# Column units of a four-layer plus two-layer transformer: high and low activations in one 512-column matmul, pooling by its band, and a reordered conformer tail

## What is computed

```python
for i in range(4):                      # kinds: retention, conformer, stick breaking, retention
    x = x + mixer_i(rms_norm(x))
    x = x + relu(rms_norm(x) @ w1) ** 2 @ w2          # hidden width 4096
x = rms_norm(x)
for layer in range(2):                  # hybrid layers
    h = rms_norm(x)
    b, c, xa, up, q, k, v, ga, gp, gt = split(h @ w_in)
    y_a = (b * conv3(c * xa)) @ w_a_out
    y_p = grouped(mean_of_window(up, 2 | 4 | 8 | 16) - up) @ w_pool * pool_scale
    y_t = windowed_attention(q, k, v, bias, sink) @ w_attn_out
    x = x + (sigmoid(ga) * y_a + sigmoid(gp) * y_p + sigmoid(gt) * y_t) @ w_o
    gate, u = split(rms_norm(x) @ w_gu)               # 2 x 2816
    x = x + (silu(gate) * u) @ w_down
out = rms_norm(x)
# conformer: a * sigmoid(gate), a causal depthwise convolution of 31 taps, layer norm, silu, a projection
```

## Time and profile before

| what | value |
|---|---|
| three executions, median (lowest to highest) | 2462.28 us (2461.33 to 2462.77) |
| the profiled execution, its own time | 2464.05 us |
| its span, first to last instruction | 2461.8 us, so 2.2 us lie around it |
| instructions in it | 35215, of them 14772 matmuls and as many weight loads |
| busy: PE, DVE, ACT | 2380.7, 1480.9, 1115.7 us |
| mean granted TensorE clock | 0.990 of 2.4 GHz |
| HBM | 421.40 MB read, 173 GB/s over the span |

### The profile page before, as it was taken

How to read it: one execution, slowest core, us unless ns; L and a number is a source line. 1 busy time by engine, 2 the same in 40 slices (tenths; PEclk the granted TensorE clock), 3 DMA queues, 4 the chain that set the end, 5 groups by cost and what they waited for, 6 DMA issues and landing times.

```text
span 2461.8 us, 35215 instructions
## 1 busy us (share of the span) xinstructions
PE 2380.7 (97%) x14772; PEld 2112.3 (86%) x14772; DVE 1480.9 (60%) x1443; ACT 1115.7 (45%) x1107; POOL 135.7 (6%) x182
## 2 busy tenths in 40 slices
PE   7999999979999899999999999999999999999998
PEld 6787998958988689877879978899899898998997
DVE  6666546966456654576564556755654567466454
ACT  5444444235436543454453445533444455334343
POOL 0000090500000000000000000000000000000000
PEclk9999999989999999999999999999999999999999
DMA  6443654214453255434545444435444454443543
GB/s 261 180 188 142 230 218 171 103 69 177 171 204 137 103 201 205 172 155 165 194 182 205 171 160 180 161 130 214 167 172 187 171 197 167 155 192 147 201 169 121
DMA packets 68369, 424.17 MB, mean 172 GB/s; under 512 B 10832, under 2 KB 11120, under 8 KB 22432
## 3 DMA queue, kind: packets, MB, share of 16 engines
q1 hardware_dynamic: 58752, 399.83, 42.0%
q0 software_dynamic: 9504, 22.71, 2.9%
HBM read 421.40 MB, written 5.28 MB: 173 GB/s over the span
## 4 chain that ended last, share of the span: by engine, by line
PE 90%; DVE 6%; ACT 3%; issue 1%; DMA 0%; POOL 0%; DVEq 0%; ACTq 0%
PE pair L695 19%; PE pair L697 18%; PE pair L696 18%; PE acc L695 10%; PE acc L696 9%; PE acc L697 9%; DVE work L1940 2%; DVE w_lo L1652 1%; PE pair L738 1%; PE acc L1067 1%; PE acc L1094 1%; PE acc L1083 1%; PE pair L1131 1%; ACT act_hi L1240 1%; PE pair L864 1%
## 5 line engine op out<-in xcount | busy, mean ns | idle before, releaser
L1652 DVE TENSOR_TENSOR w_lo<-raw,w_hi 128x2048 fp32r<-128x2048 f32 (+1 forms) x404 | 860.8, 2161 | 226.2 <-ACT w_hi L1185 225.2
L1185 ACT ACTIVATE w_hi<-raw 128x2048 fp32r<-128x2048 f32 (+1 forms) x404 | 713.1, 1804 | 156.3 <-PE acc L697 126.0
L695 PE MATMUL pair<-act_hi,w_hi 128*128 128x256 f32 x2496 | 709.9, 284 | 2.5 <-DVE w_lo L1652 2.5
L697 PE MATMUL pair<-act_hi,w_lo 128*128 128x256 f32 x2496 | 706.3, 283 | 0.0
L696 PE MATMUL pair<-act_lo,w_hi 128*128 128x256 f32 x2496 | 706.2, 283 | 0.0
L695 PEld LDWEIGHTS pair<-act_hi,w_hi 128*128 128x128 f32 x2496 | 478.7, 192 | 10.6 <-issue 8.5
L696 PEld LDWEIGHTS pair<-act_lo,w_hi 128*128 128x128 f32 x2496 | 478.8, 192 | 2.1
L697 PEld LDWEIGHTS pair<-act_hi,w_lo 128*128 128x128 f32 x2496 | 478.7, 192 | 0.0
L695 PE MATMUL acc<-w_hi,hid_hi 128*128 128x512 f32 x848 | 335.4, 396 | 6.2 <-DVE hid_lo L1705 6.2
L696 PE MATMUL acc<-w_lo,hid_hi 128*128 128x512 f32 x848 | 331.3, 391 | 0.0
L697 PE MATMUL acc<-w_hi,hid_lo 128*128 128x512 f32 x848 | 330.6, 390 | 0.0
(11 more groups left out here) (225 smaller groups left out, 2436.8 us busy)
## 6 DMA issues: line engine op xcount, KB each, us to landing
raw<-weights SPq DMA_DIRECT2D x356, 1024.0 KB, 6.6
raw<-weights SPq DMA_DIRECT2D x48, 512.0 KB, 6.3
work<-bias_scratch POOLq DMA_DIRECT2D x32, 192.0 KB, 2.8
bias_scratch<-bias_rows POOLq DMA_DIRECT2D x4, 1024.0 KB, 22.6
work<-ret_gn_w POOLq DMA_DIRECT2D x8, 256.0 KB, 5.2
work<-ret_gn_b POOLq DMA_DIRECT2D x8, 256.0 KB, 5.9
work<-table_pool POOLq DMA_DIRECT2D x2, 1024.0 KB, 7.4
work<-table_decay POOLq DMA_DIRECT2D x2, 768.0 KB, 6.7
```

What stands on the lines that cost most here:

```text
L695: mm(o, a_hi, b_hi, start=start, stop=False)
L697: return mm(o, a_lo, b_hi, start=False, stop=stop)
L1185: run(w_hi[slot][:, part], raw[slot][:, part], ACT.Copy).then_inc(hi_done, 1)
L1652: tt(w_lo[slot][:, part], raw[slot][:, part], w_hi[slot][:, part].bitcast(F32), ALU.subtract).then_inc(lo_done, 1)
```

## The change

`act_hi` and `act_lo` become two halves of one tile, `hid_hi` and `hid_lo` too. `unit_both` streams both halves against the high weights in one matmul of 512 columns and the high half against the low weights in one of 256. A pair now holds two column tiles, high and low sums side by side, so each *piece* of a unit has its own pair and the sums have to be added: ACT copies the low halves out (`low_half`), DVE adds the others (`join`). This form replaces `unit_f` in all six MLPs and for all column units of the hybrid layers, those between the heads too, but for kv and the pooling weights. The first unit's transposes move from the middle of the second unit to its first quarter. In the gated MLP the gate's half is joined first and goes through silu. In the hybrid layers the evacuations of every such unit become ACT's `low_unit` and DVE's `join_unit`, each with the rounding of the next unit's pieces in it where that is due. Pooling multiplies only by the band: 120 + 136 + 16 columns of 512. In the conformer, the mean of the first two tiles is used as a shift (`C_NEG`). DVE adds it to tiles 0 to 4 in one operation and to tile 6 within its convolution, PE to tiles 5 and 7 with the identity. PE sums seven tiles and their squares ahead of tile 6, and what is left of the mean (`C_DELTA`) is taken off behind that. PE's counts of pairs, of values and of gates are changed to match (`"p": 4` and so on). The diff, cut to its core, with 12 columns of indentation left out in most lines:

```diff
-        act_hi = sb("act_hi", [P, KT, SEQ], F32R)
-        act_lo = sb("act_lo", [P, KT, SEQ], F32R)
-        hid_hi = sb("hid_hi", [P, KT, SEQ], F32R)
-        hid_lo = sb("hid_lo", [P, KT, SEQ], F32R)
+        act = sb("act", [P, 2, KT, SEQ], F32R)
+        act_hi, act_lo = act[:, 0, :, :], act[:, 1, :, :]
+        hid_both = sb("hid", [P, 2, KT, SEQ], F32R)
+        hid_hi, hid_lo = hid_both[:, 0, :, :], hid_both[:, 1, :, :]
...
-        C_Y, C_SQ = tiles(work[:, 2304:4352]), tiles(work[:, 0:2048])
+        C_Y, C_SQ = tiles(work[:, 2304:4352]), tiles(work[:, 10240:12288])
+        C_NEG, C_DELTA, C_DSQ = (val[:, 1, a:a + SEQ] for a in (256, 512, 768))
...
+def unit_both(both=act, quarter=None, middle=None, quarters=None):
+
+    for piece in range(2):
+        o = open_pair()
+        h, l = open_piece(piece, 2 * P)
+        for n in range(2):
+            if (piece, n) == (0, 1) and quarter is not None:
+                quarter()
+            if n == 1 and quarters is not None:
+                quarters(piece)
+            b, cs = 512 * n, slice(n * P, (n + 1) * P)
+            for k in range(KT):
+                mm(tiles(o[:, b:b + 512]), h[:, k, cs], both[:, :, k, :], start=k == 0, stop=False)
+                last = mm(o[:, b:b + SEQ], l[:, k, cs], both[:, 0, k, :], start=False, stop=k == KT - 1)
+        close(last)
+        if piece == 0 and middle is not None:
+            middle()
+    S.u += 1
...
     def step(first):
-        unit_f(middle=turn_first if first else None)
+        unit_both(quarter=turn_first if first else None)
         mul_b(first, False)
-    mlp_walk(pe, S, chunks, {"u": 4, "p": 2, "c": 2}, lambda: first_unit("F"), step, lambda: mul_b(False, True))
+    mlp_walk(pe, S, chunks, {"u": 4, "p": 4, "c": 2}, lambda: first_unit("F"), step, lambda: mul_b(False, True))
...
+        if n:
+            if n == 1:
+                await_drained(shift_use)
+            last = mm(o[:, 0:SEQ], ident[:], C_NEG, start=False, stop=True)
...
+    pe.wait_ge(conv_ready, 2)
+    o = open_pair()
+    shift_use = S.p - 1
+    for k in range(2):
+        last = mm(o[:, 0:SEQ], C_MEAN, C_Y[:, k, :], start=k == 0, stop=k == 1)
...
-    order = (0, 1, 2, 4, 3, 5, 6, 7)
+    order = (5, 0, 1, 2, 3, 4, 7, 6)
     for k in order:
-        if k in convolved:
-            await_drained(convolved[k])
-        else:
-            pe.wait_ge(conv_ready, S.due("conv_ready"))
+        if k in (5, 0, 7):
+            pe.wait_ge(squared, S.due("squared"))
+        if k == 6:
+            pe.wait_ge(conv_ready, 5)
         last = mm(o[:, 0:SEQ], C_MEAN, C_Y[:, k, :], start=k == order[0], stop=k == order[-1])
-    last.then_inc(pair_full, 1)
-    o = open_pair()
-    for k in range(KT):
-        if k % 4 == 0:
+        if k == 6:
+            last.then_inc(mean_ready, 1)
             pe.wait_ge(squared, S.due("squared"))
-        last = mm(o[:, 0:SEQ], C_MEAN, C_SQ[:, k, :], start=k == 0, stop=k == KT - 1)
+        last = mm(o[:, 512:512 + SEQ], C_MEAN, C_SQ[:, k, :], start=k == order[0], stop=k == order[-1])
     last.then_inc(pair_full, 1)
     for i in range(2):
...
-    unit_f(middle=turn_first)
+    unit_both(quarter=turn_first)
     unit_kv()
-    qkv = [S.p - 3, S.p - 2, S.p - 1]
+    qkv = [S.p - 4, S.p - 3, S.p - 2, S.p - 1]
     for f in range(7):
-        unit = unit_t if f in (2, 3) else unit_f
+        unit = unit_t if f in (2, 3) else unit_both
         unit(middle=lambda: at_half(2 * f + 1), quarters=lambda piece: at_quarter(2 * f + piece))
         if f == 3:
...
+    reach = max(POOL_WINDOWS) // 2
     for i in range(2):
         o = open_pair()
         for k in range(4 * i, 4 * i + 4):
-            for s in range(2):
-                last = mm(o[:, (k % 4) * SEQ:(k % 4 + 1) * SEQ], H_UP[:, s, k * P:(k + 1) * P],
-                          H_POOL[:, k // 2, s, :], start=s == 0, stop=s == 1)
+            b = (k % 4) * SEQ
+            for s, t0, t1, start, stop in ((0, 0, P - reach, True, True), (1, P - reach, SEQ, True, False),
+                                           (0, P - reach, P + reach, False, True)):
+                last = mm(o[:, b + t0:b + t1], H_UP[:, s, k * P:(k + 1) * P],
+                          H_POOL[:, k // 2, s, t0:t1], start=start, stop=stop)
         last.then_inc(pair_full, 1)
-    unit_f()
...
+def low_half(dst):
+
+    o, _, _ = use()
+    run(tiles(dst), o[:].rearrange("p (n h t) -> p n h t", n=2, h=2)[:, :, 1, :],
+        ACT.Copy).then_inc(gate_ready, 1)
+
+def await_value():
+    S.v += 1
+    act.wait_ge(value_ready, S.at(S.v, "v"))
+
+def piece_done(piece):
+    act.wait_ge(piece_used, S.at(2 * S.u + piece + 1, "u", 2))
...
+    def make(first):
+        at = S.c % 2
+        for piece in range(2):
+            if not first:
+                split_piece(S.u + 1, piece)
+            piece_done(piece)
+            low_half(gate[:, at, 512 * piece:512 * (piece + 1)])
+        S.split += 0 if first else 1
+        S.u += 1
+        split_piece(S.u + 1, 0)
+        await_value()
+        round_chunk(hid())
+        split_piece(S.u + 1, 1)
+        S.split += 1
+        S.u += 1
+    mlp_walk(act, S, FFN1_CHUNKS, {"u": 4, "split": 4, "p": 4, "c": 2, "v": 2}, first_a, make, last_b)
+
+def last_b():
+    S.u += 1
...
+    run(C_NEG, o[:, 0:SEQ], ACT.Copy, scale=-D / (2 * P)).then_inc(done, 1)
+    load_table(WITH_SQRT)
...
+    def square(first, n=1):
+        run(C_SQ[:, first:first + n, :], C_Y[:, first:first + n, :], ACT.Square).then_inc(squared, 1)
+
     convolved(1)
+    await_drained(S.p - 1)
+    square(5)
+    act.wait_ge(centred, 1)
+    square(0, 5)
     convolved(2)
-    for i in range(2):
...
+    act.wait_ge(conv_ready, 5)
+    square(6)
+    o, _, _ = use(False)
+    act.wait_ge(mean_ready, 1)
+    run(C_DELTA, o[:, 0:SEQ], ACT.Copy).then_inc(delta_ready, 1)
+    run(C_DSQ, o[:, 0:SEQ], ACT.Square).then_inc(delta_ready, 1)
     act.wait_ge(rinv_ready, S.due("rinv_ready"))
     run(C_M, C_M, ACT.Sqrt).then_inc(rstd_ready, 1)
...
+    def low_unit(dst):
+
+        due = S.split == S.u + 1
+        for piece in range(2):
+            if due:
+                split_piece(S.u + 1, piece)
+            piece_done(piece)
+            low_half(dst[:, 512 * piece:512 * (piece + 1)])
+        S.split += 1 if due else 0
+        S.u += 1
+
+    def sigmoid(dst):
+        for piece in range(2):
+            await_value()
+        run(dst, dst, ACT.Sigmoid).then_inc(opened, 1)
...
+                low_half(slots_home(f)[:, 512:1024])
+        if slot % 2 and slot // 2 not in (2, 3):
+            piece_done(0)
+            low_half(slots_home(slot // 2)[:, 0:512])
...
+        low_unit(H_SIGP[:, i, :])
+        if i == 1:
+            ahead(S.u + 1)
...
+    low_unit(val[:, 1, :])
     for i in range(2):
-        next_unit()
-        use()
-        await_drained(S.p - 1)
-        round_chunk(hid_hi[:, four(i), :])
+        low_unit(gate[:, i, :])
+        if i == 1:
+            await_value()
+            round_chunk(hid_hi[:, four(0), :])
+    ahead(S.u + 1)
+    await_value()
+    round_chunk(hid_hi[:, four(1), :])
     for i in range(2):
+        low_unit(H_SIGA[:, i, :])
         sigmoid(H_SIGA[:, i, :])
     for i in range(2):
-        ahead(S.u + 1)
-        S.u += 1
-        use()
-        S.v += 1
-        act.wait_ge(value_ready, S.v)
-        round_chunk(act_hi[:, four(i), :], tiles(H_MERGED[:, i, :]))
+        low_unit(gate[:, i, :])
+        if i == 1:
+            await_value()
+            round_chunk(act_hi[:, four(0), :], tiles(H_MERGED[:, 0, :]))
+    ahead(S.u + 1)
+    await_value()
+    round_chunk(act_hi[:, four(1), :], tiles(H_MERGED[:, 1, :]))
...
+def join(dst, low):
+
+    o, done, _ = use()
+    await_gate()
+    return tt(tiles(dst), o[:].rearrange("p (n h t) -> p n h t", n=2, h=2)[:, :, 0, :], tiles(low),
+              ALU.add).then_inc(done, 1)
...
+            join(gate[:, at, part], gate[:, at, part])
+            await_drained(S.p - 1)
+            last = stt(val[:, at, part], gate[:, at, part], 0.0, gate[:, at, part], ALU.max, ALU.mult)
...
+                ins = stt(dst, src, w, C_NEG, ALU.mult, ALU.add)
...
+    dve.wait_ge(conv_ready, 4)
+    tt(C_Y[:, 0:5, :], C_Y[:, 0:5, :], C_NEG.unsqueeze(1).broadcast_to([P, 5, SEQ]), ALU.add).then_inc(centred, 1)
...
+    dve.wait_ge(delta_ready, 2)
+    stt(C_M, o[:, 512:512 + SEQ], EPS, C_DSQ, ALU.add, ALU.subtract).then_inc(done, 1)
...
+    def delta_off(i):
+        link(tt(C_Y[:, four(i), :], C_Y[:, four(i), :], C_DELTA.unsqueeze(1).broadcast_to([P, 4, SEQ]),
+                ALU.subtract))
+
+    def scaled(n):
+        two = slice(2 * n, 2 * n + 2)
+        tt(C_Y[:, two, :], C_Y[:, two, :], C_M.unsqueeze(1).broadcast_to([P, 2, SEQ]),
+           ALU.mult).then_inc(normed, 1)
+
+    delta_off(0)
     await_roots()
-    for i in range(2):
-        tt(C_Y[:, four(i), :], C_Y[:, four(i), :], C_M.unsqueeze(1).broadcast_to([P, 4, SEQ]),
-           ALU.mult).then_inc(normed, 1)
+    scaled(0)
+    scaled(1)
```

(115 more changed lines are left out.)

210 lines of the change are left out of this document (91 added, 119 removed).

## The result

Over 20 runs each the changed kernel took a median of 2466.04 us (2463.79 to 2467.65), the kernel before 2462.36 us (2461.33 to 2463.97): a ratio of 1.0014, 95% interval 1.0007 to 1.002. The forecast was 2447.5 and faster. What came is 3.7 us slower, within the 0.2% (4.9 us) that the prediction calls no change. 2466 lies inside the range, one microsecond from its end, where the prediction had not put its likeliest case: that it lies inside bears out no step of the forecast.

A forecast was written before the change was run, and what follows sets the result against it. PE was taken as the bound, its time the number of matmuls times their pace. -34.9 - 3.4 - 7.5 + 31.0 = -14.8 us from 2464.05 gave 2449.2, or 2447.5 for the median; range 2434 to 2467.

The forecast's parts named there:

- Part 1: Column units: 82 units pairing 512 with 256 columns take 11.10 us each instead of 11.52; -34.9 us.
- Part 2: Pooling: multiplying only by the bands takes 5.2 us, 1.7 less per layer; -3.4 us.
- Part 3: Conformer tail: 10.6 us in series plus a 1.6 us DVE operation ahead, instead of 19.8; -7.5 us.
- Parts 4 and 5: Merging halves by extra ACT copies and DVE additions, in the MLPs and between the heads: nothing added.
- Part 6: New PE waits after b1 (6.0 us) and w_a_out (5.4), slow clock, wa0 late: 15.5 per layer, +31.0 us.
- (a): In the hybrid layers the new waits are not there, rounding reaches chunk 0 in time: 2418 us; chance 0.05.
- (b): DVE becomes the bound between the heads and first results come late: 2458 to 2466 us, no change; chance 0.16.
- (c): In column units the 512-column stream from two blocks costs like two 256s: 2482 us, slower; chance 0.07.
- (d): In column units only a fixed 2.5 ns per matmul can be saved: 2476 us; chance 0.06.

The follow-up runs named there:

- f1: e4 with pooling and conformer put back as before, leaving the new form of the column units alone: 2443.86 us, 0.9921 of the kernel before.
- e1: The changed kernel with high and low part of each tile stored adjacent, so the 512 columns are one block: 2465.82 us, ratio 1.0012 to the kernel before.
- w1: The changed kernel with all matmuls of a unit 512 columns wide, low weights multiplying both halves too: 2730.79 us, ratio 1.1088 to the kernel before.
- e2: The changed kernel with all eight 512-column matmuls of a column tile first, then its eight 256s: 2457.19 us, ratio 0.9976 to the kernel before.
- g2: e4 with matmuls in groups of two, two of 512 columns and then two of 256: 2424.76 us, ratio 0.9846 to the kernel before.
- e4: The changed kernel with ACT rounding chunk 0 ahead of the second unit's first evacuation, in both loops: 2436.25 us, ratio 0.9894 to the kernel before.
- p1: The kernel before with the banded pooling alone: 2459.99 us, ratio 0.999 to the kernel before.
- c1: The kernel before with the conformer's new order alone, with its buffers and counts: 2456.01 us, ratio 0.9972 to the kernel before.
- b1: e4 with each piece's sixteen 512-column matmuls ahead of its sixteen 256s: 2423.61 us, ratio 0.9842 to the kernel before.

## Why the prediction was wrong

**Part 1 is the step that failed.** "32 x (0.227 + 0.120) = 11.10 us" adds a pace measured among 512s to one measured among 256s, for a sequence in which neither is followed by its own kind. Measured: 235 + 117 ns, a unit of 11.290 by the median, and -18.3 us in place of -34.9 (-18.6 by f1). The prediction did see that something in the sum was shown by no row, but took it for the operand in two blocks; e1 and w1 show that this costs nothing. The unknown was in the order of the widths, of which the same holds: no row before shows a 512 and a 256 in turn. That the order matters is shown by e2, which changes it alone in the kernel after, and by g2, which changes it alone in e4. Why strict alternation falls into the longer rhythm nearly always, and into the forecast's 0.347 in six of 58 units, stays open.

**The other terms hold.** Part 1's count of 82 units is right: `unit_both` issues 5248 matmuls, 82 times 64. Part 2: 1.6 us per layer in the trace, 1.7 forecast; p1 gave 2.4 of 3.4. Part 3: from DVE's last convolution to PE going on the changed kernel needs 506.79 to 516.88, 10.1 us, where the forecast had 10.6. The operation ahead takes 1.49, not 1.6, so the stage itself is 8.3 us shorter. The timeline of its tail, the counterparts of the earlier trace rows:

```profile
506.37 0.42 DVE L2098 TENSOR_TENSOR work<-work 128x256 f32<-128x256 f32 x1
...
507.39 0.61 PE L943 MATMUL pair<-work 128*128 128x256 f32 x2
...
512.41 2.08 ACT L1484 ACTIVATE val<-work,cols 128x256 f32<-128x256 f32 x4
...
516.88 0.80 PE L698 MATMUL acc<-w_hi,act 128*128 128x512 f32 x1 [8.88 <-DVE act L1799]
```

Two squares' sums on PE instead of sixteen are left in it. c1 gave 6.4, with an interval that includes both the 7.5 forecast and these 8.3. Parts 4 and 5, nothing: f1 shows none, and no wait of PE on scores or on a pair between the heads is in the list. Part 6, the largest term after part 1: from the last matmul's start to the restart 5.97 us (1670.52 to 1676.49) and 5.46 (1722.16 to 1727.62), forecast 6.0 and 5.4; DVE's idle time 10.83, forecast about 11; slow clock behind each; wa0 0.3 instead of 0.7 late; and 29.8 us came back by removing the cause of the first two. One slip is in the range: its lower end adds up to 2435 and not 2434.

**The sum again.** With the single runs: -18.6 (f1) - 2.4 (p1) - 6.4 (c1) + 29.8 (e4 against after) = +2.4 us, and +3.7 was measured; the intervals of the single runs are 2 to 4 us either way, so this agrees as well as it can. The forecast's own terms with only part 1 replaced give -18.3 - 3.4 - 7.5 + 31.0 = +1.8.

**The rivals.** (a), no waits: false, though e4 makes it true; it then takes 2436 and not 2418, again by part 1. (b), DVE between the heads: false. The time fell at the end of its 2458 to 2466, for a reason that isn't there: a number that fits supports no mechanism. (c): false in its mechanism, the two blocks, but it was the right place to doubt, and it had the right question, how much of the 13.3 ns is saved. Its threshold was put wrongly. The forecast gain of 14.8 us is 5.6 ns per 512, which is what may be *lost*; at least 7.7 of the 13.3 have to be saved. Measured are 0.223 / 32 = 7.0 ns, just too little, and this alone makes the change a loss instead of a gain. (d), the fixed part of 2.5 ns that the Trainium skill states ("TensorE: Matmul & The Clock Gate", section on where the extra 2.5 ns come from): by it part 1 would be an estimate of -6.6 us. The traces lie between it and the forecast: 7.0 ns a matmul in alternation, and 12.7 in b1 ((11.513 - 11.106) / 32). They do not agree with that figure in any order of the widths that was run.

## What to carry to other kernels

A pace read from a stretch of equal matmuls holds for equal matmuls; before widths are mixed, ask for a row that shows the mixture, and if there is none, bound it. If widths have to be mixed, keep equal ones together: here even two in a row recovered nearly all, and it is an exchange of two loops. Look at the spread of the units too, and not only at their median: here the few that ran at the forecast's pace told that it could be had. And follow each in-order queue past a moved step: one rounding that stood a few places too late, in two loops, cost 29.8 us in all, and the new form of the units is worth 18.6.
